# Shifting the moving operands against the split weights by unused SBUF buffers, in a two-layer diffusion trunk step

## What is computed

```python
u = _dwconv(h @ w_up, conv_w, conv_b)         # (256 tokens, 2048) @ (2048, 11264)
g, up = jnp.split(u, 2, axis=-1)
return (jax.nn.silu(g) * up) @ w_down         # (256, 5632) @ (5632, 2048)
```

## Time and profile before

| | |
|---|---|
| median of 3 runs | 2674.48 us (2681.84, 2650.21, 2674.48) |
| profiled execution | 2675.88 us |
| its span, first to last instruction | 2674.1 us |
| TensorE matmul busy | 2550.9 us (95%) |
| VectorE, ScalarE busy | 1485.3 us (56%), 1295.8 us (48%) |

### The profile page before, as it was taken

One profiled execution on the slowest core, in us unless ns is written; L12 is line 12 of the kernel. 1 busy time (PEld: TensorE's weight loads), 2 busy tenths in 40 slices (PEclk: granted clock), 3 DMA queues, 4 the chain that ended last, 5 costly groups with the idle time before them and its releaser, 6 DMA issues. The chain is left out here.

```text
span 2674.1 us, 52531 instructions
## 1 busy us (share of the span) xinstructions
PE 2550.9 (95%) x20826; PEld 2328.3 (87%) x20826; DVE 1485.3 (56%) x1970; ACT 1295.8 (48%) x1795; POOL 11.7 (0%) x20
## 2 busy tenths in 40 slices
PE   6799999989999999999989999789899999999997
PEld 1487988878888888899989889778899999999997
DVE  1334455655454545577765445645655565567676
ACT  1443444364444444466565444334655555556553
POOL 0000000000000000000000000000000000000000
PEclk9999999989999999999989998889899999999999
DMA  9886665768888888865646884123455555555553
GB/s 388 330 317 233 231 228 184 289 256 309 318 316 319 314 318 313 321 212 192 203 128 234 321 299 142 62 93 114 156 189 186 184 187 185 185 188 187 176 186 107
DMA packets 170060, 608.28 MB, mean 227 GB/s; under 512 B 18688, under 2 KB 25152, under 8 KB 169648
## 3 DMA queue, kind: packets, MB, share of 16 engines
q1 hardware_dynamic: 168624, 600.33, 64.0%
q10 hardware_dynamic: 512, 2.97, 0.3%
q0 software_dynamic: 768, 2.79, 0.3%
HBM read 601.38 MB, written 4.63 MB: 227 GB/s over the span
## 5 line engine op out<-in xcount | busy, mean ns | idle before, releaser
L498 DVE TENSOR_TENSOR w_lo<-raw,w_hi 128x1024 fp32r<-128x1024 f32 x756 | 925.5, 1225 | 966.3 <-ACT w_hi L491 964.6
L491 ACT ACTIVATE w_hi<-raw 128x1024 fp32r<-128x1024 f32 x756 | 798.7, 1057 | 1018.2 <-PE banks L638 994.2
L636 PE MATMUL banks<-xs_ffn,w_hi 128*128 128x256 f32 x4224 | 1188.3, 281 | 5.2 <-DVE xs_ffn L792 5.0
L637 PE MATMUL banks<-xs_ffn,w_hi 128*128 128x256 f32 x4224 | 1181.9, 280 | 0.0
L638 PE MATMUL banks<-xs_ffn,w_lo 128*128 128x256 f32 x4224 | 1181.7, 280 | 0.0
L636 PEld LDWEIGHTS banks<-xs_ffn,w_hi 128*128 128x128 f32 x4224 | 797.8, 189 | 43.5 <-issue 42.6
L638 PEld LDWEIGHTS banks<-xs_ffn,w_lo 128*128 128x128 f32 x4224 | 803.8, 190 | 0.0
L637 PEld LDWEIGHTS banks<-xs_ffn,w_hi 128*128 128x128 f32 x4224 | 795.3, 188 | 0.0
L592 PE MATMUL banks<-raw,cond 128*32 128x512 f32 x1536 | 227.2, 609 | 29.2 <-DMA raw<-in_w_mod 18.0
L636 PE MATMUL banks<-xs_even,w_hi 128*128 128x256 f32 x832 | 241.8, 291 | 10.0 <-DVE w_lo L498 5.9
L637 PE MATMUL banks<-xs_even,w_hi 128*128 128x256 f32 x832 | 233.3, 280 | 0.0
(11 more groups left out here) (305 smaller groups left out, 2054.2 us busy)
## 6 DMA issues: line engine op xcount, KB each, us to landing
raw<-in_w_mod SPq DMA_DIRECT2D x384, 512.0 KB, 6.7
raw<-in_ffn_w_up SPq DMA_DIRECT2D x352, 512.0 KB, 3.5
raw<-in_ffn_w_down SPq DMA_DIRECT2D x176, 512.0 KB, 4.1
raw<-in_even_w_in SPq DMA_DIRECT2D x72, 512.0 KB, 4.0
raw<-in_odd_w_in SPq DMA_DIRECT2D x64, 512.0 KB, 4.5
raw<-in_even_w_out SPq DMA_DIRECT2D x32, 512.0 KB, 3.7
raw<-in_odd_w_out SPq DMA_DIRECT2D x32, 512.0 KB, 3.2
raw<-in_odd_w_tail SPq DMA_DIRECT2D x8, 448.0 KB, 3.7
```

Source lines behind the costliest of these rows:

```text
L491: act.activation(w_hi[:, o % SPLIT], raw[:, s % RAW], ACT.Copy).then_inc(hi_done.sem, 1)
L498: dve.tensor_tensor(w_lo[:, o % SPLIT], raw[:, s % RAW], w_hi[:, o % SPLIT].bitcast(F32), ALU.subtract).then_inc(lo_done.sem, 1)
L636: pe.matmul(made, hi, x_hi, start=start and not second, stop=False, skip_group_check=second)
L637: pe.matmul(made, hi, x_lo, start=False, stop=False, skip_group_check=second)
```

## The change

Six buffers that nothing reads or writes are put on the stack. `stage_pad` (64 columns, 256 bytes a partition) comes behind the last buffer that lives through the whole program, so that every buffer of a stage moves up by 256 bytes. In front of the moving operands of single stages come 128 and 384 bytes more (`pad_ffn0`, `pad_ffn1`), 160 and 64 (`pad_out1b`, `pad_out1a`) and 288 (`pad_odd`). No instruction, wait or order is touched. With the distances modulo 512 that follow:

| stage | before | after |
|---|---|---|
| `xs_even` (with the output projections of layer 0) | 448 | 192 |
| `xs_ffn0` | 448 | 320 |
| `xs_odd` | 448 | 480 |
| `cq` | 448 | 192 |
| `xs_out1a` | 448 | 416 |
| `xs_out1b` | 448 | 352 |
| `xs_ffn1` | 448 | 64 |

```diff
         m0 = sb("m0", [2 * HEADS, 2])
+        stage_pad = sb("stage_pad", [P, 64])
...
             with ExitStack() as scope:
+                pad_ffn = sb(f"pad_ffn{l}", [P, (32, 96)[l]], scope=scope)
                 acts = sb(f"acts{l}", [P, KF, NT], scope=scope)
                 xs = sb(f"xs_ffn{l}", [P, KD, 2 * NT], F32R, scope)
...
+                pad_b = sb("pad_out1b", [P, 40], scope=scope)
                 xs_b = sb("xs_out1b", [P, HEADS, 2 * NT], F32R, scope)
+                pad_a = sb("pad_out1a", [P, 16], scope=scope)
                 xs_a = sb("xs_out1a", [P, HEADS, 2 * NT], F32R, scope)
...
                         with ExitStack() as inner:
+                            pad_odd = sb("pad_odd", [P, 72], scope=inner)
                             xs = sb("xs_odd", [P, KD, 2 * NT], F32R, inner)
```

## The result

After the change the median is 2702.88 us (18 runs), that of before 2653.20 us in 18 runs beside them: a ratio of 1.0149, 95% interval 1.0117 to 1.0181 (the ratios here are of means; with two groups of times on either side that of the medians is another, 1.0187). The change makes the kernel slower by 1.5%, which is within 2% and inside the range of the prediction, but on the other side of its forecast of 2667.

The account below looks back on a forecast made before the run. TensorE's pace from matmul to matmul was taken to bound the kernel. With 0 for every stage's pace and -7 us for a draw in the last block, 2675.9 became 2668.9, less 1.4 for the median: 2667.5 us, range 2618 to 2714.

Parts of the forecast that it names:

- What bounds it: Whole kernel: TensorE's time from one matmul start to the next sets the time; ScalarE, VectorE and DMA costed at 0.
- Layer 1's feed-forward at 64: Last block, 6336 matmuls, distance 448 to 64: pace change taken as 0, plus -7 us as mean of a draw.
- the row of 18 products at 64: Value products of the latent attention, at 64 before the change: 2.12 us / 18 = 117.8 ns, the slow pace.
- the row says 0: Layer 1's feed-forward: already slow, and the 18 value products at 64 are slow too, so 0 us from the pace.
- the -7: Layer 1's feed-forward: mean gain in us of a quick draw, one in four executions, 28 / 4.
- 0 for the stages other than the last: All stages before layer 1's feed-forward: each restart draws its pace again as now, so 0 us.
- All slow: All split stages: at 64, 192 and 320 every restart ends slow; +31 us, 2706 us; chance 0.20.
- A third pace: Both feed-forward blocks: a slower pace of 122.2 ns, three meetings of the reads; +75, 2750 us; chance 0.09.
- All quick: All split stages: new distances keep weight load and moving read apart at every restart; -47 us, 2627 us; chance 0.16.
- a pace below 113: At least one long block: some distance has no meeting of the reads, 108.9 ns; 2550 to 2638 us; chance 0.13.
- the distance cannot matter: All split stages: by the skill's separate TensorE read ports, time follows the draws, about 2667, with or without pads.

## Why the prediction was right and wrong

*What bounds it* held. No instruction more, no other work on ScalarE, VectorE or DMA, their slack larger, and the time follows the pace of TensorE alone. The two paces, 113.3 and 117.8, and the 28 us between them in the last block are confirmed: the runs fall in two groups 25 to 28 us apart, and profiles at 448 show that block at either pace.

*Layer 1's feed-forward at 64* was right in its pace: the row of 18 products at 64 said 117.8 and the block ran at 117.8, so "the row says 0" stood at +0.4. Wrong was the -7 put beside it. It took a quick draw to be as likely at 64 as at 448, and one in four; at 448 it was eleven in 18 here, and after the change both profiles have the block slow but for 14 runs of three in one (two of 18 times, 2675.98, may be quick draws). The three runs of before were too few to size a draw, and the prediction started from a median that is 21 us above that of 18 runs. Between typical runs of the two kernels, about 2650 and 2703, the last block is by this reading the largest single loss, some 28 us, though it is 0 between the two profiles.

*The step that failed* is "0 for the stages other than the last: each restart draws again, as it does now, and no row here shows which way another distance would lean". At 448 and 192 a restart can end at either pace, though in ffn0 the order of the two is the same in every execution and no draw. At 320, 352, 416 and 480 it ends slow or slower: in the profile after no run of three there is quick. In place of 0 the runs show 18.6 (ffn0) + 6.6 (odd) + 3.6 (out1a and out1b) = 28.8 us by the paces, 26.1 with the waits counted in. There was a row that leaned: the same 18 products, all slow, at 64. I used it for the one stage that went to 64. That 64 and 320 are one distance, since the pattern repeats after 256, no row of before could tell.

*All slow* (0.20, 2706) came nearest in size: +31 foretold, +25.4 measured between the profiles. Its forecast of the stages is half right, and its reason, where in the stream the two reads meet, no run tested. At 64 and 320 nearly every profiled stretch is slow, as it said (the most that was quick is 28% of odd, with all stages at 320). But it wanted 192 slow too, for +6 in even, and 192 is the twin of 448; and it gave odd and out1b 117.8, where 480 and 352 have 118.3 and 120.0.

*A third pace* (0.09) exists, at 119.4 to 120.0 on the multiples of 128, and 121 to 122 beside 112; its price was guessed at 122.2. The change only put one into the 384 matmuls of out1b. *All quick* (0.16) and *a pace below 113* (0.13) did not occur: the lowest mean of any stage at any distance is 113.3.

The rule of the Trainium skill, "SBUF — State Buffer", "Who interferes with whom", that weight load and moving operand have read ports of their own, was weighed there as "the distance cannot matter". Moving the weights alone by 128 bytes costs 50 us between the medians (2700.76 against 2650.55) and 1.2% by the ratio of means, so for these products the measurement decides against what was drawn from it: it does matter.

What makes the pace is argued and not shown. That a weight load runs under the matmul ahead of it, and that the two read the same partitions, makes a meeting of their reads the plain guess, since in the long stages only the difference of the two addresses counts. No run takes the weight loads away or shows which of the two stands. What picks the pace at a restart is open too, and why it then holds, in the last block for 700 us.

## What to carry to other kernels

Where TensorE is busy from end to end and a window gives two paces for one shape at a full clock, the placing of stationary against moving operand is a knob: here 112 instead of 448 bytes (modulo 256: 112 instead of 192) gave 0.9% and one group of times instead of two, and a wrong one cost 1.5 to 3.4% (the 3.4 in a single execution). Scan it with one execution per setting and several stages at different distances in each, since the paces of the stages then add up to the time. Before you call a mix of paces a draw, lay two executions side by side: in ffn0 the order was the same. And size a real draw from some 15 runs, not three: with two groups 28 us apart a median of three can stand on either.

## What the runs showed of the hardware

- Matmuls of 256 float32r columns with a weight load each take from 113.3 to 122.2 ns at clock 1.00, by the distance of the two operands and, at some distances, by the stretch: 119.4 to 120.0 at 0, 128 and 256; 113.3 or 117.8 at 192 and 448; 117.8 in the feed-forward blocks at 64 and 320, but for one short quick stretch in three of the four profiles; 116.7 to 118.6 at 32, 416, 480 and 496.
- The pattern repeats after 256 bytes (192 and 448, 64 and 320, 112 and 368; the last pair less exactly, 113.3 to 114.3 against 115.2 in 384 matmuls). It was not seen in every small stage: out1b has 113.3 at 448 and 117.8 at 192.
- It is fine: 112 takes 113.6 in ffn0, 120 takes 121.5 and 104 takes 120.0.
- A stretch can take its pace at its start and hold it: at 448 the same 600 us hold 5097 matmuls in one execution and 5297 in another. In ffn0 the order of quick and slow stretches is the same in four executions, but for one of 56.
- At 112 the slow pace does not hold in the feed-forward blocks: a slow start goes over to the quick pace after four runs of three at the most. At 448 it held for 2054.
